# Weight-cast DMAs ordered after a tile's write instead of reading it, and biases split once as small arrays kept in memory

## Time and profile before

| | us |
|---|---|
| median of 3 runs | 3105.2 (3101.47, 3105.20, 3110.16) |
| the profiled execution's own time | 3091.35 |
| span of its slowest core (core 7) | 3089.8 |
| spans of cores 0 to 7 | 3057.6, 3012.1, 3038.0, 3016.0, 3053.5, 3084.5, 3071.2, 3089.8 |
| PE busy on core 7 | 1970.0 (64%) |
| DVE, ACT, POOL busy | 1047.7 (34%), 658.1 (21%), 458.8 (15%) |
| mean granted PE clock, all cores | 0.814 to 0.819 of full |

### The profile page before, as it was taken

How to read it: one execution, slowest core, us unless ns; L and a number is a source line. 1 busy time by engine, 2 the same in 40 slices (tenths; PEclk the granted TensorE clock), 3 DMA queues, 4 the chain that set the end, 5 groups by cost and what they waited for, 6 DMA issues and landing times.

```text
span 3089.8 us, 41430 instructions; the slowest of 8 cores (3012.1 to 3089.8 us)
## 1 busy us (share of the span) xinstructions
PE 1970.0 (64%) x16141; PEld 1237.2 (40%) x16141; DVE 1047.7 (34%) x1459; ACT 658.1 (21%) x971; POOL 458.8 (15%) x567
## 2 busy tenths in 40 slices
PE   3879999946980545676741886267971434676730
PEld 2445555513550434455530343134551433555520
DVE  4212121166444111222214665154543111222258
ACT  1000100162220212222211343153220111222210
POOL 0000000000002213343310000000003212234300
PEclk9989999978995768889875898557995877789865
DMA  7399776915336999787868683999346999889876
GB/s 132 48 152 125 103 104 91 111 37 132 137 97 124 219 226 210 198 179 198 214 154 214 191 223 82 132 110 189 149 122 123 224 201 210 200 187 191 179 230 272
DMA packets 99377, 495.95 MB, mean 161 GB/s; under 512 B 40864, under 2 KB 41504, under 8 KB 49664
## 3 DMA queue, kind: packets, MB, share of 16 engines
q0 software_dynamic: 76672, 304.57, 58.1%
q1 hardware_dynamic: 22512, 188.72, 17.2%
HBM read 904.23 MB, written 205.47 MB: 359 GB/s over the span
## 4 chain that ended last, share of the span: by engine, by line
PE 50%; DMA 16%; another core or an unknown queue 13%; DVE 8%; issue 7%; ACT 4%; POOL 1%; DVEq 0%; ACTq 0%; SPq 0%; POOLq 0%
PE ps L752 9%; PE ps L899 8%; PE ps L446 7%; PE ps L762 6%; DMA wex<-w 4%; PE ps L921 4%; PE ps L924 4%; PE ps L1098 4%; DMA wbf<-w 3%; DMA cq_yb<-ysc 2%; PE ps L418 2%; PE ps L732 2%; DMA tbl<-g_rec,g_row 2%; DMA xs<-xe 2%
## 5 line engine op out<-in xcount | busy, mean ns | idle before, releaser
L752 PE MATMUL ps<-xT,wex 128*128 128x128 bf16 x6208 | 409.3, 233 | 229.3 <-DMA wex<-w 220.7
L752 PEld LDWEIGHTS ps<-xT,wex 128*128 128x128 bf16 x6208 | 400.2, 106 | 267.2 <-issue 257.0
L762 PE MATMUL ps<-wex,hid 128*128 128x512 bf16 x776 | 232.4, 453 | 155.5 <-DVE hid L757 146.8
L770 DVE TENSOR_SCALAR y<-ps,g_tabs 128x512 f32<-128x512 f32 x194 | 139.1, 748 | 420.7 <-ACT y L768 293.7
L899 PE MATMUL ps<-yb,diag 128*128 128x512 bf16 (+1 forms) x1488 | 262.3, 334 | 17.2 <-DVE yb L940 14.8
L732 PE MATMUL ps<-cb_sb,xg 128*128 128x128 bf16 x1552 | 115.9, 223 | 178.3 <-DMA xg<-hrow,g_itok 133.8
L768 ACT ACTIVATE y<-ps,g_tabs 128x512 f32<-128x512 f32 x194 | 133.4, 688 | 392.9 <-DMA ysc<-y,g_idst 300.6
L757 DVE TENSOR_TENSOR hid<-ps,sa 128x256 bf16<-128x256 f32 x97 | 41.2, 424 | 467.6 <-ACT sa L755 437.5
L899 PEld LDWEIGHTS ps<-yb,diag 128*128 128x128 bf16 x1488 | 135.8, 98 | 137.8 <-issue 18.2
L762 PEld LDWEIGHTS ps<-wex,hid 128*128 128x128 bf16 x776 | 78.9, 110 | 270.0 <-issue 222.5
L157 POOL DMA_DIRECT2D wex<-w x135 | 74.8, 573 | 654.0 <-PE ps L446 350.0
(11 more groups left out here) (209 smaller groups left out, 2582.8 us busy)
## 6 DMA issues: line engine op xcount, KB each, us to landing
wex<-w POOLq DMA_DIRECT2D x135, 1024.0 KB
wbf<-w POOLq DMA_DIRECT2D x57, 1024.0 KB, 20.0
wex<-wbf SPq DMA_DIRECT2D x19, 3072.0 KB
hres<-rt SPq DMA_DIRECT2D x17, 1024.0 KB, 4.0
wsl<-win POOLq DMA_DIRECT2D x16, 1024.0 KB, 11.8
rt<-xe SPq DMA_DIRECT2D x9, 1024.0 KB, 4.9
cq_h<-hres SPq DMA_DIRECT2D x9, 1024.0 KB, 11.2
cq_ya<-ysc SPq DMA_DIRECT2D x9, 1024.0 KB, 7.5
```

Source lines behind the costliest of these rows:

```text
L752: S.group(PE, [lambda e, kc=kc: e.matmul(PH[:, c:c + 128], lhsT=w13[:, kc, c:c + 128], rhs=xt[:, kc, :], start=(kc == 0), stop=(kc == NJ - ...
L762: S.group(PE, [lambda e, f=f: e.matmul(P[:, :], lhsT=hd[:, f, :], rhs=w2[:, f, q * 512:(q + 1) * 512], start=(f == 0), stop=(f == 1)) for ...
L770: S.op(DVE, lambda e: e.tensor_scalar(out=dst, in0=P[:, :], scalar1=gate, scalar2=None, op0=ALU.mult), **kw)
```

## The change

Two things. First, `dma` and `copy` get a new argument `after`: the DMA waits for the last writes of those buffers, but isn't recorded as their reader, and `convert` uses it instead of `reads`. Secondly, the three calls of `bias_split` are replaced. `split_biases`, called once at the start, loads all three biases as one float32 array of 128 by 52 (26.6 KB), splits them into three bf16 parts in five DVE instructions (three casts, two subtractions) of 52 columns, and writes the parts to a small array `bdr` in memory with nine DMAs on SP. `load_bias`, called in the three old places, loads three rows (12 or 15 KB) from there to a tile of three partitions on SP. The bias matmuls use three rows of the ones and of `bsp` instead of 128. The masks `m3` and the padded inputs go. Cut to its core:

```diff
+    def dma(self, eng, fn, key, reads=(), writes=(), accw=(), cont=False, after=()):
...
+        for b in after:
+
+            deps.extend(b.w.values())
         self._wait(eng, deps)
...
-    def bias_split(i, off, scr, src, w):
...
+    bdr, B_bdr = dtmp("bdr", [3, NBIAS], BF16)
+
+    def split_biases(scr):
+
+        w = NBIAS // 128
+        b, Bf = M.put("bsrc", [128, w], scr)
+        t, Bt = M.put("bpart", [128, 3, w], scr + 256, BF16)
+        S.copy(SP, b[:], bias_d[:, :], 'bias', writes=[Bf])
         for r in range(3):
+            S.op(DVE, lambda e: e.tensor_copy(out=t[:, r, :], in_=b[:]), reads=[Bf], writes=[Bt] if r == 0 else [], accw=[] if r == 0 else [Bt])
             if r < 2:
+                S.op(DVE, lambda e: e.tensor_tensor(out=b[:], in0=b[:], in1=t[:, r, :], op=ALU.subtract), reads=[Bt], writes=[Bf])
+        for r in range(3):
+            for a, c in BSEG:
+                S.copy(SP, bdr[r:r + 1, a:a + c].rearrange("o (p x) -> (o p) x", p=128), t[:, r, a // 128:(a + c) // 128], 'bdr',
+                       reads=[Bt], accw=[B_bdr], cont=True)
+
+    def load_bias(i, off):
+        a, c = BSEG[i]
+        t, Bt = M.put(f"bsp{i}", [3, c], off, BF16)
+        S.copy(SP, t[:, :], bdr[:, a:a + c], 'bias', reads=[B_bdr], writes=[Bt])
+        return t, Bt
...
-                S.group(PE, [lambda e: e.matmul(P[0:n, :], lhsT=ones[:, 0:n], rhs=bsp[:, q * 512:(q + 1) * 512], start=True, stop=False)] +
+                S.group(PE, [lambda e: e.matmul(P[0:n, :], lhsT=ones[0:3, 0:n], rhs=bsp[0:3, q * 512:(q + 1) * 512], start=True, stop=False)] +
...
             S.copy(POOL, wbf[l][k * 128:(k + 1) * 128, c * 4096:(c + 1) * 4096], third(l, CVT[l][k], c), f'cv{(k * 3 + c) % 2}',
-                   reads=list(after), accw=[B_wbf[l][k]])
+                   accw=[B_wbf[l][k]], after=after)
...
-    bsp, B_bsp = bias_split(0, BSP0, P0 + 38400, bias_d[0], D)
+    split_biases(P0 + 38400)
+    bsp, B_bsp = load_bias(0, BSP0)
...
-            bsq, B_bsq = bias_split(2, BSQ0, P0 + 38400, biasq_d[:, :], 2560)
+            bsq, B_bsq = load_bias(2, BSQ0)
...
-        S.group(PE, [lambda e: e.matmul(P[:, :], lhsT=ones, rhs=bsq[:, b * 512:(b + 1) * 512], start=True, stop=False)] +
+        S.group(PE, [lambda e: e.matmul(P[:, :], lhsT=ones[0:3, :], rhs=bsq[0:3, b * 512:(b + 1) * 512], start=True, stop=False)] +
...
-    bsp, B_bsp = bias_split(1, BSP0, P0 + 38400, bias_d[1], D)
+    bsp, B_bsp = load_bias(1, BSP0)
```

More of the change, by code:

```diff
@@ L139, in group @@
         self._mark((eng.sem, eng.cnt), reads, writes, accw)
-    def dma(self, eng, fn, key, reads=(), writes=(), accw=(), cont=False):
+    def dma(self, eng, fn, key, reads=(), writes=(), accw=(), cont=False, after=()):
         if key not in self.dsems:
@@ L154, in dma, with copy @@
         self._mark((s, s.cnt), reads, writes, accw)
-    def copy(self, eng, out, in_, key, reads=(), writes=(), accw=(), cont=False):
-        self.dma(eng, lambda e: e.dma_start(out=out, in_=in_), key, reads, writes, accw, cont)
+    def copy(self, eng, out, in_, key, reads=(), writes=(), accw=(), cont=False, after=()):
+        self.dma(eng, lambda e: e.dma_start(out=out, in_=in_), key, reads, writes, accw, cont, after)
     def gather(self, out, table, idx, bound, key, reads=(), writes=(), accw=(), cont=False):
@@ L226 @@
         [('snkb', 32), ('cst', 160), ('wdw', 16 * 31), ('padmask', 160), ('brb0', 36), ('brb1', 36),
-         ('thr', NTHR), ('iota', 32), ('jota', 18), ('pidx', 1), ('vmask', 1), ('vbig', 1), ('m3', 3),
+         ('thr', NTHR), ('iota', 32), ('jota', 18), ('pidx', 1), ('vmask', 1), ('vbig', 1),
          ('tok0', 10), ('tok1', 8)]:
@@ L234 @@
 NCB = 768
+NBIAS = 2 * D + 2560
+BSEG = ((0, D), (D, D), (2 * D, 2560))
 GB_NAMES = ['mix0', 'ffn0', 'mix1', 'ffn1']
@@ L249, in build @@
     gb_d = din("gb", [4, 2, 128, D])
-    bias_d = din("bias", [2, 128, D])
+    bias_d = din("bias", [128, NBIAS // 128])
     win_d = din("win", [NJ, 128, 4096])
@@ L259, in build @@
     wq_d = din("wq", [128, NJ * D])
-    biasq_d = din("biasq", [128, 2560])
     wo_d = din("wo", [128, NJ * D])
@@ L333, in stream @@
         return load
-    def bias_split(i, off, scr, src, w):
[L337 to L341, removed]
-        for r in range(3):
[L343 to L350, removed]
-            if r < 2:
-                S.op(DVE, lambda e: e.tensor_tensor(out=b[:], in0=b[:], in1=p[:], op=ALU.subtract), reads=[Bp], writes=[Bf])
-        S.op(DVE, lambda e: e.tensor_copy(out=bsp[:], in_=t[:]), reads=[Bt], writes=[Bb])
-        return bsp, Bb
+    bdr, B_bdr = dtmp("bdr", [3, NBIAS], BF16)
[4 more added lines that the diff above has]
+        S.copy(SP, b[:], bias_d[:, :], 'bias', writes=[Bf])
+        for r in range(3):
+            S.op(DVE, lambda e: e.tensor_copy(out=t[:, r, :], in_=b[:]), reads=[Bf], writes=[Bt] if r == 0 else [], accw=[] if r == 0 else [Bt])
+            if r < 2:
+                S.op(DVE, lambda e: e.tensor_tensor(out=b[:], in0=b[:], in1=t[:, r, :], op=ALU.subtract), reads=[Bt], writes=[Bf])
[8 more added lines that the diff above has]
+        return t, Bt
     def load_gb(name, off):
@@ L1366, in prepare @@
     shared['gb'] = gb
[L1367 to L1373, removed]
+    segs = [f('conv_b_out')[0], f('b_o')[0], np.concatenate([f('b_k'), f('b_v'), f('b_q')[0][perm]])]
+    shared['bias'] = np.ascontiguousarray(np.concatenate([v.reshape(128, -1) for v in segs], 1))
     cfp = np.zeros((128, NCF), np.float32)
@@ L1398, in prepare @@
     put('vbig', (pp >= 16).astype(np.float32) * OOB)
-    put('m3', (pp == np.arange(3)[None]).astype(np.float32))
     put('tok0', pp + np.array([row0(0, i) for i in range(10)], np.float32)[None])
```

## The result

The changed kernel takes **3077.2 us** (median of 5 runs, 3065.2 to 3112.0) where the kernel before, measured beside it, takes 3107.5 (5 runs, 3101.5 to 3114.5): a ratio of 0.9874, 95% interval 0.9838 to 0.9909. That is 39 us faster (0.0126 x 3107.5), about half of the 76 forecast, and outside the range of 3008 to 3062. A second measurement, on another chip, gave 0.9906 [0.9864, 0.9948], 29 us. The profiled execution took 3112.0 us. Times are medians of all executions and ratios compare only those in which no die was slowed, so a ratio can differ a little from the quotient of the times beside it.

The account below looks back on a forecast made before the run. No engine bounds the whole program, so each edit was judged by what ends last in its stage. 21 + 11.0 + 52.9 + 2.2 - 11 = 76 us off 3105.2 gave 3029 us, range 3008 to 3062.

Parts of the forecast that it names:

- The start, 21 us: Before the first convolution: 14.8 us of PE idle, 2.2 of slow matmuls and 4 of x loading go, 21 us.
- Ahead of attention, 11 us: Before attention: the bias split's DVE instructions and load go, so ACT's wait for the meta scores goes, 11.0 us.
- The casts' wait, 52.9 + 2.2 us: In attention: ACT's long wait for a cast goes, 52.9 us, and its 12 other waits give 2.2 us.
- Cost 0, at worst 15 ns x 114 = 2 us: Bias matmuls: weight loads of three rows cost nothing, at worst 2 us, left out of the sum.
- the collision: Layer-1 mixer_out: later casts delay the bet_mix load, 11 us given back, not growing with the number of casts behind.
- The backlog: End of attention: the last cast is issued near 2094, 44 us after bet_mix.
- one of the signs named: Casts at the end of attention: the prediction is wrong if their spacing rises from 9.5 us.
- The bound of 22 us: Layer-1 mixer_out: upper bound of the collision's price, twice the 11 us taken, since the casts last longer.
- The rival of a bigger collision: Layer-1 mixer_out: rt, gam_mix and bet_mix all meet a full queue, wait 35 us or more, 3055 us; 17%.
- No collision: Layer-1 mixer_out: the last casts leave room and bet_mix lands in time, 3018 us; 14%.
- slower: Layer-1 mixer_out: residual tiles starve beside the casts, each of eight costs 12 us more, 3114 us; 3%.
- the long piece isn't the casts': In attention: another wait takes the long piece's place, only 32 us from the bias parts are left, 3073 us; 5%.

Follow-up runs that it names:

- e4: The changed kernel with a zeroed 128-partition bias tile, three rows loaded, and bias matmuls reading 128 rows again: 3040.4 us, ratio 0.9825 to the kernel before.
- e2: The kernel before with only the casts ordered after the write instead of reading the tile, biases as before: 3072.1 us, ratio 0.9948.
- e6: The kernel before with one edit, bias matmuls reading three rows instead of 128: 3114.2 us, ratio 1.0069.
- e7: e4 with seven of attention's 16 casts held until bet_mix has landed in layer-1 mixer_out: 3031.0 us, ratio 0.976 to the kernel before.

## Why the prediction was half right

**The start, 21 us: right.** Every part of it shows: 14.77 and 2.2 us in the rows above, the x stage ending 60.86 - 57.40 = 3.5 us earlier where 4 were taken, 21.4 in all at the second convolution group, 20 to 21 in the stage means. The Trainium skill's warning of writes under 512 B ("DMA: Bandwidth & Descriptors", Specifications) didn't decide here: the nine writes landed in 19 us, and the first matmul that needs them comes some 600 us later. Whether the small pieces are the reason for the 19 us, no run here shows.

**Ahead of attention, 11 us: right.** e4 against e2, which differ only in how the biases are made, have q stage and attention at 485.4 and 497.5, 12.1 us.

**The casts' wait, 52.9 + 2.2 us: right on core 7, too much for the mean.** There attention fell from 217.0 to 147.7, 69.3 us with the 11 and the 3.7 us of the mark: 65.6 where 66.1 were worked out. In the mean of the eight cores it is 209.5 - 147.7 - 3.7 = 58.1. e2 has the casts' part alone: 217.0 - 163.2 = 53.8 on core 7 and 209.5 - 162.9 = 46.6 in the mean, where 55.1 were worked out. That is no loss by itself: core 7 also pays more in `mixer_out` (182.4 to 214.5, 32.1 us, against 26.0 in the mean), and the two together are worth 21.7 us on core 7 and 20.6 in the mean. The forecast was made for core 7, the slowest in the profile before; in the first measurement it isn't the slowest.

**Failed: "Cost 0, at worst 15 ns x 114 = 2 us".** The three-row matmuls cost 21 us in e6, ten times the upper end. The load's duration was no trouble (90 ns against 98), but the pace was: 0.2 us more per column block, 114 blocks, 24 us at most. I priced the instruction and took for granted that it stays hidden. The 16-row loads of the earlier trace rows stood in a stream of their own kind; they bounded what such a load lasts, not what it does between 128-row ones. The Trainium skill says that the load's time depends on its columns, not on its rows ("TensorE: Matmul & The Clock Gate", section on LDWEIGHTS). The trace agrees for the duration within a tenth (98 ns with 128 rows, 90 with 3), and e6 shows that no pace follows from it.

**Failed: the collision, "-11", "by that rule the delay doesn't grow with the number of casts behind".** It was 29 us in the stage means, of which 25 to 26 are the casts' (e4, e2). The backlog was foreseen (last cast 55 us after `bet_mix` for the 44 forecast; once `mixer_out` had begun the casts' spacing rose from 9.5 to 10 to 14 us, one of the signs named). The queues do share the engines, as the rule says: 787 packets of q0 beside 738 of q1. The step that failed is the next one, from "interleaved" to "doesn't grow". On core 1 before, the last cast was issued beside `bet_mix` (2043.00, 2043.24) and POOL saw it landed at 2064.57, halfway through the flight of 45.0 us. Up to then q0 and q1 moved 212 and 261 packets; after it, beside the first expert loads, 222 and 496. After the change the casts lasted to the end of the flight and beyond. SP's opening loads, `gam_mix` and `bet_mix` behind three other transfers, then ran at 30.8% of the engines: that is a rate, and the flight grows for as long as the casts last, up to the 64 us worked out under e7. The bound of 22 us was twice one core's price where it should have been the stage's opening loads over the share that the casts leave. The rival of a bigger collision (17%, 3055) was the one that came true here; the three-row matmuls took the time beyond it.

**The sum.** 21 + 11 + 47 (e2's mean) - 21 - 26 = 32 us, against 39 and 29 measured (0.9874, 0.9906). On core 7, for which the forecast was made, with e2's terms for it: 21 + 11 + 54 - 21 - 32 = 33. Of the 76, 21 went to the three-row matmuls and 21 to the larger collision there; the casts' wait was right to 1.3 us. (In the mean the shortfall of 44 splits into 21, 15 and, for the shorter wait of the earlier cores, 8.)

**The other rivals.** No collision, slower, and "the long piece isn't the casts'" are out: e2 and the ACT rows. The one that ended slower had its place right (the layer-1 mixer) and its mechanism wrong: residual tiles waited 9.9 us once, not eight times.

**Open.** Why a weight load of 64 rows or fewer isn't hidden between 128-row loads, where 100 are: only 3, 64, 100 and 128 rows were run. Also open is why the q stage pays more per block than `mixer_out`, and what holding the casts is worth for the whole program, beyond its stage.

## What to carry to other kernels

Price an instruction that gets smaller by the pace of the stream around it, not by its duration: a bias matmul of three rows did a fortieth of the work and cost 0.2 us more than one of 128. When a wait is taken from background copies, look at what they will run beside next, and price each critical load there at the share of the engines that the copies leave; here holding the copies back for the two opening loads gave 32 us in that stage. And take a term's gain and its price from the same core: core 7 gained more from the casts than the mean and paid more for them.

## What was not expected of the hardware

- A weight load of 3 or 64 rows among 128-row ones isn't overlapped: 3.88 us per block of 17 matmuls in place of 3.68; at 100 rows 3.68. Its own duration falls from 98 to 90 ns (3 rows).
- POOL's queue, two DRAM-to-DRAM casts in flight, holds 70.0% of the 16 engines against 30.8% for SP's loads (787 and 738 packets), and stretches a 1 MB load to 63.7 us from 20.6 (e7).
- Nine writes of pieces of 32 and 40 bytes took 19 us to land beside a full DMA; SP alone waited for them, with nothing urgent behind.
